# One VectorE operation with two factors in place of two ScalarE operations for the diagonal block of each fetched expert

## The reference

```
def one_block(hb):
    ...
    top_s, pos = lax.top_k(cand, PEER_TOPK)
    idx = jnp.take_along_axis(cand_idx, pos, axis=-1)
    g = jax.nn.softmax(top_s, axis=-1).astype(hb.dtype)
    u = jnp.take(expert_u, idx, axis=0)
    act = jax.nn.gelu(jnp.einsum("thkd,td->thk", u, hb))
    vv = jnp.take(expert_v, idx, axis=0)
    return jnp.einsum("thk,thkd->td", g * act, vv)
```

## Time and profile before

| what | us |
|---|---|
| median of 3 runs | 2083.92 (2081.96 to 2084.43) |
| the profiled execution's own time | 2089.93 |
| its span, first to last instruction | 2088.1 |
| PE busy | 1679.8 (80%) |
| DVE busy | 1219.0 (58%) |
| ACT busy | 706.8 (34%) |
| POOL busy | 610.2 (29%) |
| DMA of fetches, share of 16 engines | 70.8% |

### The profile page before, as it was taken

How to read it: one execution, slowest core, us unless ns; L and a number is a source line. 1 busy time by engine, 2 the same in 40 slices (tenths; PEclk the granted TensorE clock), 3 DMA queues, 4 the chain that set the end, 5 groups by cost and what they waited for, 6 DMA issues and landing times.

```text
span 2088.1 us, 22263 instructions
## 1 busy us (share of the span) xinstructions
PE 1679.8 (80%) x7420; PEld 763.0 (37%) x7420; DVE 1219.0 (58%) x3172; ACT 706.8 (34%) x2204; POOL 610.2 (29%) x584
## 2 busy tenths in 40 slices
PE   5899998599788997979957787767777767877776
PEld 2775897444453544445421221121121111211211
DVE  2434216856764563448757777767777765554554
ACT  2225202123873332233323333333333343333332
POOL 0000000033323332322234443435443444334331
PEclk7999999799879999999979999999999999999999
DMA  9455613299868998978949999999999999999996
GB/s 399 180 197 208 255 42 120 82 412 415 352 250 345 369 421 354 402 312 326 310 190 422 421 421 421 421 421 420 422 422 421 421 420 398 422 422 422 422 421 262
DMA packets 102467, 718.50 MB, mean 344 GB/s; under 512 B 13584, under 2 KB 13584, under 8 KB 15696
## 3 DMA queue, kind: packets, MB, share of 16 engines
q0 software_dynamic: 82944, 604.02, 70.8%
q1 hardware_dynamic: 18544, 110.69, 13.6%
q10 hardware_dynamic: 864, 2.36, 0.3%
HBM read 712.30 MB, written 4.73 MB: 343 GB/s over the span
## 4 chain that ended last, share of the span: by engine, by line
DMA 42%; PE 33%; DVE 13%; issue 6%; ACT 3%; POOL 2%; SPq 0%; DVEq 0%; POOLq 0%; ACTq 0%
DMA ring<-in_expert_uv_dram,uidx 41%; PE ps L797 8%; PE ps L540 7%; PE ps L659 6%; DVE ring L1437 4%; POOL ring L415 2%; PE ps L680 2%; PE ps L665 2%; PE ps L536 1%; PE ps L512 1%; PE ps L720 1%; DMA ring<-in_wpack_dram 1%; PE ps L570 1%; PE ps L603 1%; PE ps L495 1%
## 5 line engine op out<-in xcount | busy, mean ns | idle before, releaser
L797 PE MATMUL ps<-ring,wdiag 128*32 128x512 f32 x2304 | 851.8, 634 | 237.5 <-ACT wdiag L1049 212.6
L415 POOL DMA_INDIRECT ring<-in_expert_uv_dram,uidx x576 | 608.9, 1057 | 1394.7 <-PE ps L797 955.8
L1437 DVE CUSTOM_DVE_ANT_0 ring<-ring,mA 128x1024 f32<-128x1024 f32 x576 | 700.9, 1223 | 474.1 <-DMA ring<-in_expert_uv_dram,uidx 458.5
L797 PEld LDWEIGHTS ps<-ring,wdiag 128*32 128x32 f32 x2304 | 171.8, 114 | 864.1 <-ACT wdiag L1049 518.3
L1042 ACT ACTIVATE gel<-act_in 128x1 f32<-128x1 f32 x576 | 116.8, 203 | 855.2 <-DVE act_in L1437 845.3
L1049 ACT ACTIVATE wdiag<-repeat,wsel 128x32 f32<-128x32 f32 x576 | 185.2, 321 | 18.9
L1044 ACT ACTIVATE wsel<-gel,gsel 128x1 f32<-128x1 f32 x576 | 169.7, 295 | 18.7
L540 PE MATMUL ps<-hB,ring 128*128 128x384 f32 x320 | 108.8, 492 | 0.0
L720 PE MATMUL ps<-hB,ring 128*128 128x384 f32 x256 | 90.2, 505 | 8.5 <-issue 8.5
L659 PE MATMUL ps<-hB,ring 128*128 128x384 f32 x256 | 88.5, 501 | 1.8 <-DVE kv L1278 1.8
L540 PEld LDWEIGHTS ps<-hB,ring 128*128 128x128 f32 x320 | 59.1, 190 | 42.1 <-issue 5.2
(11 more groups left out here) (233 smaller groups left out, 1602.5 us busy)
## 6 DMA issues: line engine op xcount, KB each, us to landing
ring<-in_wpack_dram SPq DMA_DIRECT2D x96, 1024.0 KB, 9.3
ring<-in_expert_uv_dram,uidx POOLq DMA_INDIRECT x576
xB<-in_x_b_dram SPq DMA_DIRECT2D x2, 1536.0 KB, 18.5
o_y_p<-mA ACTq DMA_DIRECT2D x16, 128.0 KB
bias<-in_bias_dram SPq DMA_DIRECT2D x1, 1024.0 KB, 32.4
o_v_p<-kv SPq DMA_DIRECT2D x4, 256.0 KB
o_k_p<-xB SPq DMA_DIRECT2D x4, 256.0 KB
xB<-in_keysT_dram SPq DMA_DIRECT2D x1, 1024.0 KB, 8.3
```

What stands on the lines that cost most here:

```text
L415: nc.gpsimd.indirect_dma_start(out=ring[:, slot, :], out_offset=None, in_=ins["expert_uv"], in_offset=bass.IndirectOffsetOnAxis(ap=uidx[:, ...
L797: mm = nc.tensor.matmul(pY[c * GT:(c + 1) * GT, half, :], wdiag[:, n % NDIAG, :], ring[:, ROW[n][0], D + half * 512:D + (half + 1) * 512], ...
L1437: nc.vector.tensor_tensor_reduce(r, r, h2n[:, g % 2, :], 1.0, 0.0, ALU.mult, ALU.add, act_in[:, g % 2, j:j + 1]).then_inc(s["dot"], 1)
```

## The change

ACT keeps only the gelu of a fetch. `wsel` and its semaphore are gone. The block `wdiag` is made by DVE in one operation that multiplies `repeat` by two per-partition factors, the gelu and the softmax weight. DVE does it in entry ("gather", n+1), ahead of `dot(n+1)`, and waits there for ACT's gelu of fetch n, for the placed weights of the block (first fetch of a block only) and for fold n-8.

```
                 def spread(n):
                     g, j = n // GT, n % GT
                     act.wait_ge(s["dot"], n + 1)
-                    p, a = TILES[g]
-                    if j == 0:
-                        act.wait_ge(s["placed_kept"], p + 1)
                     nc.scalar.activation(gel[:, j:j + 1], act_in[:, g % 2, j:j + 1], ACT.Gelu_apprx_tanh).then_inc(s["gelu"], 1)
-                    act.wait_ge(s["gelu"], n + 1)
-                    nc.scalar.activation(wsel[:, j:j + 1], gel[:, j:j + 1], ACT.Identity,
-                                         scale=gsel[:, p % 2, a, j:j + 1]).then_inc(s["weight"], 1)
-                    act.wait_ge(s["weight"], n + 1)
-                    if n >= NDIAG:
-                        act.wait_ge(s["fold"], n - NDIAG + 1)
-                    nc.scalar.activation(wdiag[:, n % NDIAG, :], repeat[:, :], ACT.Identity,
-                                         scale=wsel[:, j:j + 1]).then_inc(s["diag"], 1)
...
+                def diagonal(n):
+                    g, j = n // GT, n % GT
+                    p, a = TILES[g]
+                    dve.wait_ge(s["gelu"], n + 1)
+                    if j == 0 and a == 0:
+                        dve.wait_ge(s["placed_kept"], p + 1)
+                    if n >= NDIAG:
+                        dve.wait_ge(s["fold"], n - NDIAG + 1)
+                    nc.vector.tensor_scalar(wdiag[:, n % NDIAG, :], repeat[:, :], gel[:, j:j + 1], gsel[:, p % 2, a, j:j + 1],
+                                            ALU.mult, ALU.mult).then_inc(s["diag"], 1)
...
                 def gather(n):
+                    if 1 <= n <= NG * GT:
+                        diagonal(n - 1)
                     if n < NG * GT:
                         dot(n)
```

More of the change, by code:

```diff
@@ L266 @@
          "shifted", "exp", "picked", "placed", "placed_kept",
-         "h2", "h2_kept", "dot", "gelu", "weight", "diag", "fold", "sum_kept", "joined", "scaled", "natural", "added", "stored",
+         "h2", "h2_kept", "dot", "gelu", "diag", "fold", "sum_kept", "joined", "scaled", "natural", "added", "stored",
          "gate_ps", "gate_sb", "v_out", "k_out", "conv_out", "chain"]
@@ L360, in program @@
         gel = sb("gel", [P, GT])
-        wsel = sb("wsel", [P, GT])
         wdiag = sb("wdiag", [P, NDIAG, GT])
```

## The result

The change made the kernel slower: 2115.66 us (median of 5 runs, 2111.98 to 2118.77) against 2081.96 us (2079.99 to 2084.43) for the kernel before on the same chip. The ratio is 1.0159, with a 95% interval from 1.0141 to 1.0177. That is +33.7 us, where +18 was forecast (2102, range 2086 to 2120).

What follows compares the result with a forecast made beforehand. Bounds were taken by stage: PE, then hand-overs between engines in attention, PE with DMA, and full DMA from 1080 us. 3 + 12 - 1.5 + 5 + 0 - 0.5 = +18 on 2083.9 gave 2102 us, range 2086 to 2120.

Steps and rivals of the forecast that it cites:

- Attention: 521 to 630 us: VectorE and ScalarE wait for each other in a longer loop; +12 us (-1 to +18).
- the hand-over at the end: Kernel's end: gelu to fold takes 0.59 us instead of 0.94, a gain of 0.35; stage term -0.5 us.
- a loop of 9.0 us a pair: Attention: each of 12 pairs of ticks takes 9.0 us, 108 us in all, without a wait for PE.
- PE's lateness: Attention: DVE's 19.0 us of waiting for PE's scores; two thirds, 13 us, was kept on top of 108.
- 416 to 521 us: Stage with PE full: blocks behind the convolution (+2.1 us) and a top-k piece (0.9) delay PE; +3 (0 to +5).
- Merge and projection: 630 to 921 us: four folds right behind `wdiag` win 0.35 us each; -1.5 us (-4 to +3).
- Retrieval ticks: 921 to 1080 us: folds 144 to 147 wait for the first pick, later picks start later; +5 us (+1 to +9).
- the other picks: 921 to 1080 us: dearer dots ahead of later picks cost about +0.5 us a pick for four picks.
- Last stage: 1080 us to the end: DMA stays full, 0.57 us of waiting a fetch covers 0.48 added; 0 us.
- ACT's relief: Rival, attention: ScalarE's saved work comes off the path, 9 us and up to 4 more, 2071 us; 10%.
- Hidden: Rival: PE's lateness absorbs attention's longer loop (-1 us), no change that can be told, 2084 to 2088 us; 13%.
- VectorE as bound of the last stage through GpSimd's port: Rival: waiting for GpSimd's instructions makes 0.68 us a fetch added against 0.57 of cover; 2117 to 2130 us; 7%.

Runs made afterwards that it cites:

- e1: The changed kernel, but fetches 33 to 65 (attention) handed on the old way by ScalarE's three operations; 2096.23 us, ratio 1.0063 to the kernel before.
- e2: The changed kernel, but only fetches 33 to 65 (attention) use VectorE's one operation, all others ScalarE as before; 2100.59 us, ratio 1.0075 to the kernel before.
- e3: The changed kernel with the block of fetch n ahead of the dot of n+2 in place of n+1; 2147.05 us, ratio 1.0294 to the kernel before.
- e5: The changed kernel with the block of fetch n right behind the dot of n+1, not ahead of it; 2116.16 us, ratio 1.0133 to the kernel before.
- e10: The changed kernel, but the eight fetches ahead of the eight picks handed on by ScalarE's three operations; 2112.97 us, ratio 1.0138 to the kernel before.
- e11: The kernel before with four tiny VectorE memsets behind each dot from fetch 450 on; 2089.0 us, ratio 1.0025 to the kernel before.
- e12: The kernel before with four tiny ScalarE copies behind each hand-over from fetch 450 on; 2082.27 us, ratio 0.9991 to the kernel before.
- e8: Against the changed kernel: VectorE multiplies in eight softmax weights per operation ahead, ScalarE makes gelu and one multiplication; 2086.9 us, ratio 0.9975 to the kernel before.
- e7: The changed kernel with the softmax weight as a repeated second tensor operand (scalar_tensor_tensor), not a second pointer; 2119.39 us, ratio 1.0136 to the kernel before.

## Why the prediction was right, and where it was short

**Direction and main mechanism: right; size: short.** The change cost 33.7 us where +18 was forecast, inside the stated range. Attention lost 12 to 14 us (14 by the means) where +12 was forecast, by the mechanism it named: VectorE idle ahead of the block until the gelu (38.5 us in 18 waits), shown by e1, e2, e3 and e5. The new operation's median is 0.30 us, as priced, the hand-over at the end gave the 0.35 us, and ACT is down by 706.8 - 357.5 = 349 us (355 forecast).

**How attention's +12 came about was not as worked out.** The step read: a loop of 9.0 us a pair "without a single wait for PE", and two thirds (13 us) of PE's lateness on top. In the changed kernel VectorE's wait for PE's scores is 0.7 us: none of the lateness survived. The loop itself is longer: the twelve exponential table loads stand on average 9.8 us apart (before 8.8). What the loop left out is seen in ACT's timeline of one pair:

```profile
571.94 0.61 ACT L925 ACTIVATE xB<-xB,stat 128x384 f32<-128x384 f32 x1 [2.61 <-DVE stat L1232]
...
572.56 0.56 ACT L934 COPY qB<-ps 128x512 f32<-128x512 f32 x1
...
573.27 0.88 PE L586 MATMUL ps<-ident,xB 128*128 128x128 f32 x3 [2.22 <-ACT qB L934]
...
574.18 0.48 ACT L946 COPY xB<-ps 128x384 f32<-128x384 f32 x1 [1.06 <-PE ps L586]
...
574.67 1.28 ACT L1038 ACT_TABLE_LOAD   x1
...
575.97 0.20 ACT L1038 ACTIVATE gel<-act_in 128x1 f32<-128x1 f32 x1
576.21 0.30 DVE L1436 TENSOR_SCALAR wdiag<-repeat,gel,gsel 128x32 f32<-128x32 f32 x1 [4.30 <-ACT gel L1038]
```

Between the exponential and the table load ACT also copies an output and waits for PE's transposes of its own exponentials. The lock-step has three partners, not two: VectorE waits 4.30 us for a gelu of 0.20 that stands behind ACT's wait for PE. Two errors of opposite sign made nearly the right sum; that the +12 came out is in part luck.

**416 to 521 us: right in size** (+2.5 for +3). The named cause, the block of fetch 27 behind the convolution, was forecast at +2.1 us. PE's timeline in the changed kernel has it:

```profile
501.77 2.75 PE L796 MATMUL ps<-ring,wdiag 128*32 128x512 f32 x12
506.78 2.35 PE L796 MATMUL ps<-ring,wdiag 128*32 128x512 f32 x4 [2.26 <-DVE wdiag L1436]
```

PE stands 2.26 us until the block, which VectorE begins at 506.42, behind the convolution's last copy. e3, which puts the blocks later still, made the stretch 14 us longer than before; e5's 4 us are 1.4 over the changed kernel's, within the scatter.

**Merge and projection: wrong sign**, +2 to +3 for -1.5. I gave PE a direct hand-over where it stands behind `wdiag`, and nothing back for the blocks that now stand behind VectorE's ticks. e3 lengthened this stretch by 7 us with a later block. Which single folds lose the 2 or 3 us stays open.

**Retrieval ticks: right**, 4 to 8 us for +5. The fold of 147 waited 3.39 us for the end of the first pick, as forecast, and e10, which removes that wait, took 4.6 us less than the changed kernel's trace and 1.7 less than e1's. Whether the other picks, sized at 0.5 us each for four of them, cost more than that is within the scatter.

**Last stage: the term that was put at nothing and was not.** It read "**0**", on the ground that VectorE's slack of 0.57 us a fetch covers 0.48 and a queue of ten fetches stands behind it. The cover held: DMA share 1.01 as before. But the stage lost 6 us all the same, since VectorE's longer instruction stream makes more fetches late by 0.96 us, whatever its slack (e11, e12, and the table). At first I read these 6 us from a gap in DMA behind the last `place` (a mean of 371 GB/s over dots 430 to 450, before 397), but those 20 fetches took 50.2 us, no more than before (51.3): that reading fell.

**The remainder.** +18 was forecast; of the missing 16 us, by the means of the traces, 6 are the last stage, 4.5 merge and projection, 2 attention and 1 the retrieval's ticks, whose term was read from a trace that is 4 us longer there than the others. The last 2 or 3 are within the scatter.

**The rivals.** ACT's relief did not decide: its 349 us came off the engine and none off the time. e8, with one ScalarE operation less and no new wait on VectorE, is 5 us faster; that relief is the reason is not shown, as no trace tells where the 5 us are. Hidden: refuted, since the lateness of PE that could hide the loop was used up. VectorE as bound of the last stage through GpSimd's port: the contention exists (0.24 us in 102 of 576), but taking it away (e7) changed nothing that can be told.

## What to carry to other kernels

When an operation moves to the engine that runs ahead, count what stands behind its new wait, not what it takes: here 0.30 us of work a fetch was free in attention as long as VectorE had a wait for PE to lay it in (e3), and the wait for a 0.20 us gelu cost 13 us in 33 fetches. Follow the loop through every engine that the releaser itself waits for. Before moving a product to another engine, look for the factor that is known early and multiply it in ahead, many at a time; that removed ScalarE's operation with no new dependence on its result and was the only version that was faster.

## What the hardware did that was not expected

In a stage that is bound by DMA, instructions on VectorE cost time although VectorE stands idle: 500 memsets of 0.06 us, all of them inside waits for data, cost 3.9 us, in steps of 0.96 us a late fetch, while 500 copies of 0.19 us on ScalarE cost nothing. The Trainium skill (Runtime: NRT & Kernel Launch, Instruction fetch mechanics) says that each engine streams its instructions through a DMA queue of its own in blocks, and that crossing a block is mostly hidden. The traces agree with the blocks (an instruction packet 1.5 to 2.4 us ahead of each late fetch, every 127 to 130 VectorE instructions in four of the kernels) and not with the hiding, where fetches fill all DMA engines. A queue for each engine is not to be seen: the profile lists the added packets of e11 and of e12 both under q14.
